# DeltaNet block inverse: crossing products on the two off-diagonal 64x64 array tiles, in banks of their own

## The chip, the cores and the metric

One core of a Trainium2 chip runs the whole program. The metric is the device time of one launch in microseconds (us). The engines are TensorE (PE; its weight loads have rows of their own, PEld), VectorE (DVE), ScalarE (ACT), GpSimd (POOL) and SyncE (SP), which mostly issues transfers. They run side by side and meet only at semaphores.

## The reference, cut to what matters

One inference step of a four-layer trunk in float32. Layers 0 and 3 mix tokens with a bidirectional chunked gated DeltaNet. Per head, per direction and per chunk of 64 tokens it solves a unit lower triangular 64x64 system:

```python
kb = k * beta[..., None]
a = jnp.where(strict, jnp.einsum('bhnid,bhnjd->bhnij', kb, k) * decay, 0.0)
lower = a + jnp.eye(c, dtype=a.dtype)                       # c = 64
rhs = jnp.concatenate([v * beta[..., None], kb * jnp.exp(g)[..., None]], axis=-1)
sol = lax.linalg.triangular_solve(lower, rhs, left_side=True, lower=True, unit_diagonal=True)
```

There are 8 heads of 128 channels. The context tokens (128) and the latent tokens (128) are two groups `g`, each of two chunks, and two directions `d` run over each. So one head has 2 directions x 2 groups x 2 chunks = 8 systems.

## The kernel before

The inverse of each 64x64 matrix is built by doubling. Six levels (`LEV = 6`) take blocks of 1, 2, 4, ... 32 rows to blocks twice as large. For one head the eight matrices lie in tiles of 128 partitions: combination `c = 2*d + g` picks one of four column strips of 64, and the chunk picks the partitions, rows 0 to 63 or 64 to 127. `UT(l, w)[:, 0]` holds the inverse so far (called T here), `UT(l, w)[:, 1]` its transpose (U). `AT` is the system matrix, `MW` the masked product of a level.

The heads go in pairs (`PAIRS = 4`), two heads (h0 and h1 below) at a time, each step for h0 and then for h1. One level is four steps per head:

- `s_w(lev)` (PE, L894): 8 products 64x64, `AT` by T, into PSUM bank `X`. It waits for ACT's copy of T.
- `s_m(lev)` (DVE, L2087): one operation 128x256, the bank times the level's mask, into `MW`.
- `s_ut(lev)` (PE, L902): 8 products that add to T and 8 that add to U, all accumulated in bank `Y`. The last level leaves T out.
- ACT's `s_ut(lev)` (L1586): one copy 128x512 of `Y` into `UT` (128x256 at the first and the last level).

PE's order within a level is s_w h0, s_w h1, s_ut h0, s_ut h1. Every one of these products reads partitions `r` and writes partitions `r`, with `r` the lower or upper half in turn. In the 128x128 array that uses the two diagonal 64x64 tiles (lower to lower, upper to upper) and never the two crossing ones (lower to upper, upper to lower). A float32 product is recorded as two passes, so an operation with 8 products has 16 records.

Around the levels, for the next pair and the one that ends:

- `s_gc` (PE, L855): 8 transposes that spread the decay of the next pair, after level 4. `s_dec` (DVE, L2056) makes 8 operations of it, both heads ahead of `s_m(5)`; ACT's `s_qe` then takes the exponentials.
- `s_kk`, `s_ks` (PE): key products of the next pair, which wait for ACT's last copy of the old one. `s_qd` (DVE, L2070 to L2085): scales them into `AT`, makes the first `MW` in two operations 64x256, one for each half of the partitions (L2079), and the first U. `s_r0` (DVE, L2064) reads bank `ZB` = 1.
- `s_y`, `s_z`, `s_tz`, `s_o` (PE) finish the old pair. `s_z` is the one step whose products cross (a 64x64 block of `AT` from one half into the other half, 128 columns wide); `s_v` (DVE, L2096, L2097) is between `s_tz` and `s_o`. `s_t(h)` (PE) starts T and U of the new pair from `s_qd`'s result.

Every queue is a fixed order written out by hand. The scratch of this stage lies in the weight ring, so that hardly any weights stream while it runs.

Of the kernel before, what the change touches and what calls it, by code (L numbers as in the profile page):

```python
# [7 lines left out]
ALU = mybir.AluOpType  # L8
# [4 lines left out]
P = 128  # L13
# [5 lines left out]
H = 8  # L19
# [10 lines left out]
LEV = 6  # L30
# [135 lines left out]
def trunk(nc, a, outs):  # L166
    y_p, y_s, new_dn, new_k, new_v = outs
    with ExitStack() as ctx:
# [132 lines left out]
        d_dec, d_qd, d_m, d_r0, d_v = (sem("d_" + n) for n in ("dec", "qd", "m", "r0", "v"))  # L301
# [23 lines left out]
        PAIRS, ZB = H // 2, 1  # L325
# [56 lines left out]
        def UT(l, p): return scratch(l, 2560 * p + 1536, 2, 4, HB)  # L382
        def MM(l, p): return scratch(l, 2560 * p + 2048, 4, P)
# [283 lines left out]
        def _(pe):  # L667
# [101 lines left out]
            def deltanet(l):  # L769
# [110 lines left out]
                def utps(Y, half, c, r):  # L880
                    x = HB * (4 * half + c)
                    return ps[r, Y, x:x + HB]

                def s_t(h, w, hd, X, Y):
                    pe.wait_ge(d_qd, hd + 1)
                    pe.wait_ge(a_qe, hd + 1)
                    t = UT(l, w)[:, 1]
                    for c, r in blocks():
                        mm(utps(Y, 0, c, r), t[r, c, :], identc[r, :], c == 0, False, skip_group_check=True)
                    for c, r in blocks():  # L890
                        ins = mm(utps(Y, 1, c, r), identc[r, :], t[r, c, :], False, False, skip_group_check=True)
# [73 lines left out]
                for j in range(PAIRS + 1):  # L965
# [519 lines left out]
        def _(act):  # L1485
# [59 lines left out]
            def deltanet(l):  # L1545
# [991 lines left out]
```

## Time and profile before

| | us |
|---|---|
| median of 3 runs | 2280.64 (2274.31 to 2280.94) |
| the profiled execution, its own time | 2278.45 |
| its span | 2276.6 |
| PE busy | 2180.7 (96%) |
| DVE busy | 736.2 (32%) |
| ACT busy | 390.9 (17%) |
| all 64x64 products at L669, `ring` by `ring`, x4192 records | 180.2 |

The span is one execution as the hardware profiler saw it, and the views below are of it. All times in them count from the span's start. The granted clock of TensorE was 0.983 on average. A PE record lasts some 200 ns because the result has to drain through the array, while the next one starts long before: what a stream of products costs is read from the distance between starts, not from the mean duration.

### The profile page before, as it was taken

The page shows a single profiled execution, that of the slowest core. Times are in us where ns is not written, and L with a number is a line of the kernel's source. Part 1 is how long each engine was busy: PE and PEld are TensorE (multiplying, and loading weights), DVE is VectorE, ACT ScalarE, POOL GpSimd, SP SyncE. Part 2 cuts the span into 40 slices and gives each one's busy share as a digit, 9 for nine tenths or more (in the row PEclk, how much of TensorE's full clock was granted, in tenths as well). Part 3 has the DMA queues.
Part 4 walks back from the last instruction along what each step waited for, and adds up shares of the span by engine and source line. Part 5 has one row for each costly group of instructions (what it writes and reads, how often), then busy time and mean ns, then how long its engine had stood idle before and what let it go on. Part 6 is the DMA issues. An engine that isn't in the chain of part 4 may idle for free.

```text
span 2276.6 us, 44025 instructions
## 1 busy us (share of the span) xinstructions
PE 2180.7 (96%) x19461; PEld 1657.0 (73%) x19461; DVE 736.2 (32%) x1576; ACT 390.9 (17%) x794; POOL 127.1 (6%) x221
## 2 busy tenths in 40 slices
PE   7998989999999999999999999999988899999998
PEld 4776878888888746646687788888878876466465
DVE  2234434777412300000212355562344333000002
ACT  1133441000101000000132210002143330000001
POOL 4000010111000000000000011110000000000000
PEclk8999999999999999999999999999999999999999
DMA  9973029997455699999755799563530057999992
GB/s 337 268 251 101 12 90 322 335 305 257 149 185 194 204 386 383 381 381 379 248 156 191 259 346 286 199 193 95 157 121 7 12 208 256 387 383 380 379 383 113
DMA packets 363975, 550.92 MB, mean 242 GB/s; under 512 B 12176, under 2 KB 312080, under 8 KB 358464
## 3 DMA queue, kind: packets, MB, share of 16 engines
q1 hardware_dynamic: 336288, 466.59, 59.6%
q0 software_dynamic: 21968, 76.84, 10.3%
q10 hardware_dynamic: 5536, 4.73, 0.6%
q8 instruction: 154, 2.52, 0.5%
q14 instruction: 29, 0.24, 0.0%
HBM read 537.64 MB, written 14.93 MB: 243 GB/s over the span
## 4 chain that ended last, share of the span: by engine, by line
PE 76%; SPq 11%; DVE 5%; DMA 4%; ACT 2%; issue 2%; ACTq 0%; DVEq 0%
PE ps L669 73%; SPq L494 7%; SPq L498 3%; DMA work<-in_ada_w 2%; ACT ring L1495 2%; DMA ring<-in_moe_w_down 1%; DVE ring L2056 1%; DVE work L1915 1%; ACT work L1495 1%; DVE ring L2074 0%; DVE ring L2079 0%; DVE ring L2064 0%; DMA ring<-in_ada_w 0%; PE ps L1184 0%; DVE hT L1925 0%
## 5 line engine op out<-in xcount | busy, mean ns | idle before, releaser
L669 PE MATMUL ps<-hT,ring 128*128 128x256 f32 x3200 | 715.7, 383 | 2.9 <-DVE hT L1925 2.5
L669 PE MATMUL ps<-ring,work 128*32 128x384 f32 (+7 forms) x8008 | 693.9, 438 | 17.8 <-ACT work L1495 5.4
L669 PEld LDWEIGHTS ps<-hT,ring 128*128 128x128 f32 x3200 | 609.8, 192 | 115.7 <-issue 21.4
L669 PEld LDWEIGHTS ps<-ring,work 128*32 128x32 f32 (+2 forms) x8008 | 392.6, 115 | 296.9 <-issue 180.6
L1495 ACT ACTIVATE work<-ps 128x256 f32<-128x256 f32 (+6 forms) x220 | 100.5, 467 | 1329.9 <-PE ps L669 1143.8
L669 PE MATMUL ps<-work,ring 128*128 128x256 f32 (+1 forms) x1344 | 283.9, 370 | 0.0
L669 PEld LDWEIGHTS ps<-work,ring 128*128 128x128 f32 (+1 forms) x1344 | 238.6, 185 | 34.0 <-issue 1.7
L2478 DVE SCALAR_TENSOR_TENSOR work<-work,csil 128x1024 f32<-128x1024 f32 x196 | 239.7, 1279 | 39.5 <-DMA work<-in_ada_w 39.3
L669 PE MATMUL ps<-ring 64*64 64x64 f32 (+1 forms) x4192 | 180.2, 230 | 25.4 <-ACT ring L1495 11.1
L669 PEld LDWEIGHTS ps<-ring 64*64 64x64 f32 x4192 | 159.3, 139 | 38.8 <-ACT ring L1495 17.5
L1495 ACT ACTIVATE ring<-ps 128x512 f32<-128x512 f32 (+3 forms) x208 | 101.6, 491 | 306.0 <-PE ps L669 295.8
L669 PE MATMUL ps<-work 128*128 128x128 f32 (+2 forms) x736 | 104.9, 293 | 3.4 <-DVE work L2253 3.3
L669 PEld LDWEIGHTS ps<-work 128*128 128x128 f32 (+1 forms) x736 | 94.0, 199 | 14.3 <-issue 10.3
L2400 DVE TENSOR_TENSOR work<-work,ps 128x384 f32<-128x384 f32 (+1 forms) x24 | 13.3, 553 | 248.6 <-PE ps L669 230.8
L596 POOL DMA_DIRECT2D work<-in_ada_w x112 | 60.2, 538 | 453.4 <-DVE work L2478 260.4
L1933 DVE SCALAR_TENSOR_TENSOR xT<-ps,mods,xT 128x128 f32<-128x128 f32 x160 | 43.6, 343 | 107.8 <-PE ps L669 98.7
L2090 DVE TENSOR_TENSOR ring<-ps,cst 128x256 f32<-128x256 f32 x80 | 33.3, 423 | 93.0 <-PE ps L669 92.7
L1950 DVE TENSOR_SCALAR ring<-ring,par 128x256 f32<-128x256 f32 x48 | 14.8, 352 | 135.2 <-ACT ring L1495 135.2
L669 PE MATMUL ps<-ring,cst 64*64 64x64 f32 (+1 forms) x320 | 46.9, 322 | 8.4 <-ACT ring L1495 8.4
L2461 DVE TENSOR_TENSOR work<-work,ps 128x256 f32<-128x256 f32 x44 | 18.4, 418 | 107.4 <-ACT work L1495 107.4
L2347 DVE COPY work<-ps 128x512 f32<-128x512 f32 x16 | 11.1, 692 | 117.9 <-PE ps L669 117.9
L614 POOL TENSOR_TENSOR tick<-work 1x1 f32<-1x1 f32 x2 | 0.4, 183 | 874.3 <-DMA y_rows<-work 874.3
(266 smaller groups left out, 1076.1 us busy)
## 6 DMA issues: line engine op xcount, KB each, us to landing
ring<-in_moe_w_gu SPq DMA_DIRECT2D x96, 1536.0 KB, 16.0
ring<-in_moe_w_down SPq DMA_DIRECT2D x48, 1536.0 KB, 16.6
work<-in_ada_w POOLq DMA_DIRECT2D x112, 512.0 KB, 6.5
ring<-in_ff_w_gu SPq DMA_DIRECT2D x88, 512.0 KB, 7.7
ring<-in_ada_w SPq DMA_DIRECT2D x40, 1024.0 KB, 8.7
ring<-in_dn_w_in SPq DMA_DIRECT2D x32, 1024.0 KB, 5.5
ring<-in_moe_w_gu SPq DMA_DIRECT2D x32, 1024.0 KB, 8.9
ring<-in_ff_w_down SPq DMA_DIRECT2D x44, 512.0 KB, 9.2
```

What stands on the lines that cost most here:

```text
L494: sp.dma_start(ring[:, x, 0:KC * width].rearrange("p (k n) -> p k n", k=KC), gu[e, :, c:c + width].rearrange("e (k p) n -> p (e k) n", p=P ...
L498: sp.dma_start(ring[:, x, at:at + n * DM].rearrange("p (c n) -> p c n", c=n), dn[e, c * P:(c + n) * P, :].rearrange("e (c p) n -> p (e c) ...
L596: po.dma_start(piece[b], a["ada_w"][third // ADA_T, k * P:(k + 1) * P, c:c + 1024]) \
L669: return pe.matmul(out, lhsT, rhs, start=start, stop=stop, **kw)
L1495: return act.activation(out, in_, fn, **kw)
L1915: tt(mixT[:, 2 * b:2 * b + 2, :], xT[:, 2 * b:2 * b + 2, :], rstd[:, None, :].to_broadcast([P, 2, NT]), ALU.mult).then_inc(d_nx, 1)
L1933: ins = stt(xT[:, k, g * P:(g + 1) * P], ps[:, bank, c * NT + g * P:c * NT + (g + 1) * P], mods[:, l, col + k, g:g + 1], xT[:, k, g * P:(g ...
L1950: ins = ts(v(ys[c]), x, ws[c](tap), None, ALU.mult)
L2056: ins = stt(TT(l, w)[:, 2 * d + g, :], ps4(X)[:, 2 * d + g, :], col(GC, d, g, h), cap[:, d, :], ALU.subtract, ALU.min)
L2090: tt(four(MW(l, w)), ps[:, X, 0:4 * HB].rearrange("p (d g n) -> p d g n", d=2, g=2), level(lev), ALU.mult).then_inc(d_m, 1)
L2461: tt(act_s[:, j % 3, :], gate_s[:, j % 3, :], ps[:, FB[j % 3], NT:2 * NT], ALU.mult) \
L2478: ins = stt(t, piece[b], c, t, ALU.mult, ALU.add)
```

## The change

- In each head one of the two directions is called crossed (`crossed_d`: direction 1 in even pairs, 0 in odd ones), the other straight. For the crossed direction T stays in the half of its own block, while U and `MW` of that block are kept in the other half of the partitions. The products of the crossed direction in `s_w` (T's half to the other) and for T in `s_ut` (the other half back to T's) then run on the crossing array tiles. They are written to a bank of their own, `crossing(p)` = 1 or 4 for h0 or h1, while the straight ones go to `X` and `Y`. The code issues crossing and straight products in turn. The products for U are all on the diagonal tiles as before.
- T of the crossed direction is no longer accumulated in PSUM: DVE adds it (`s_crossed`, 128x128, one per head and level 0 to 4), with a new semaphore `d_t` that `s_w` also waits for. ACT copies 128x384 where it copied 128x512.
- The last copy of U (ACT) puts the crossed blocks back in their own half: three operations, 64x128, 64x128 and 128x128, where there was one of 128x256.
- The first `MW` in `s_qd` takes four operations 64x128 where there were two of 64x256.
- `s_gc` of the next pair moves from after level 4 to after level 3. `s_dec` is split: h0 ahead of `s_m(4)`, h1 ahead of `s_m(5)`.
- Bank numbers move: `X` = 0, 2, 3 or 5, `Y` = 6 or 7, and `ZB` = 4, which is also h1's crossing bank; so `s_t` of h1 waits for `d_r0` too.

```diff
-        PAIRS, ZB = H // 2, 1
+        PAIRS, ZB = H // 2, 4
...
-            return h, 2 * (j % 2) + p, H * DN_LAYERS.index(l) + h, (2, 6)[j % 2] + p, 4 + p
+            return h, 2 * (j % 2) + p, H * DN_LAYERS.index(l) + h, 3 * p + 2 * (j % 2), 6 + p
...
+        def crossed_d(h):
+
+            return 1 - (h // 2) % 2
+
+        def crossing(p):
+            return 3 * p + 1
...
                 def s_t(h, w, hd, X, Y):
                     pe.wait_ge(d_qd, hd + 1)
                     pe.wait_ge(a_qe, hd + 1)
+                    if h % 2:
+                        pe.wait_ge(d_r0, hd + 1)
                     t = UT(l, w)[:, 1]
+                    for c, r, x in crossed(h):
+                        mm(t_crossed(h, c, r), t[x, c, :], identc[x, :])
+                    for n, (c, r) in enumerate(straight(h)):
+                        mm(t_straight(Y, c, r), t[r, c, :], identc[r, :], n < 2, False, skip_group_check=True)
...
                         pe.wait_ge(a_ut, nth(hd, lev - 1, LEV))
-                        for c, r in blocks():
-                            ins = mm(ps[r, X, HB * c:HB * c + HB], AT(l, w)[r, c, r], UT(l, w)[r, 0, c, :])
+                        pe.wait_ge(d_t, nth(hd, lev - 1, LEV - 1))
+                        for (c, r, x), (c2, r2) in zip(crossed(h), straight(h)):
+                            at = HB * (c % 2)
+                            mm(ps[x, crossing(h % 2), at:at + HB], AT(l, w)[r, c, r], t_of(h, w, c, r))
+                            ins = mm(ps[r2, X, at:at + HB], AT(l, w)[r2, c2, r2], t_of(h, w, c2, r2))
...
-                            for c, r in blocks():
-                                mm(utps(Y, 0, c, r), UT(l, w)[r, 1, c, :], MW(l, w)[r, c, :], False, False,
+                            for (c, r, x), (c2, r2) in zip(crossed(h), straight(h)):
+                                mm(t_crossed(h, c, r), UT(l, w)[x, 1, c, :], MW(l, w)[x, c, :])
+                                mm(t_straight(Y, c2, r2), UT(l, w)[r2, 1, c2, :], MW(l, w)[r2, c2, :], False, False,
                                    skip_group_check=True)
...
-                        if lev == LEV - 2 and j + 1 < PAIRS:
+                        if lev == LEV - 3 and j + 1 < PAIRS:
                             both(s_gc, j + 1)
...
+                        if lev < LEV - 1:
+                            x = 4 * HB if lev == 0 else 8 * HB
+                            f(u[:, 2 * HB:x], ps[:, Y, 2 * HB:x], ACT.Copy).then_inc(a_ut, 1)
+                            return
+                        x, y = (2 * HB * (2 + d) for d in (crossed_d(h), 1 - crossed_d(h)))
+                        for r, r2 in zip(ROWS_OF, ROWS_OF[::-1]):
+                            f(u[r, x:x + 2 * HB], ps[r2, Y, x:x + 2 * HB], ACT.Copy)
+                        f(u[:, y:y + 2 * HB], ps[:, Y, y:y + 2 * HB], ACT.Copy).then_inc(a_ut, 1)
...
+                    for d in range(2):
+                        for b, r in enumerate(ROWS_OF):
+                            to = ROWS_OF[1 - b] if d == crossed_d(h) else r
+                            ins = tt(MW(l, w)[to, 2 * d:2 * d + 2], AT(l, w)[r, 2 * d:2 * d + 2, r],
+                                     level(0)[r, d], ALU.mult)
...
+                def s_crossed(lev):
+                    def f(h, w, hd, X, Y):
+                        dve.wait_ge(p_ut, nth(hd, lev, LEV))
+                        t, new = UTF(l, w)[:, 0:2 * HB], ps[:, crossing(h % 2), 2 * HB:4 * HB]
+                        ins = tt(t, t, new, ALU.add) if lev else cp(t, new)
+                        ins.then_inc(d_t, 1)
...
+                        s_crossed(0)(*head(l, j, 0))
                     if j > 0:
                         both(s_v, j - 1)
+                    if j < PAIRS:
+                        s_crossed(0)(*head(l, j, 1))
                     for lev in range(1, LEV if j < PAIRS else 1):
-                        if lev == LEV - 1 and j + 1 < PAIRS:
-                            both(s_dec, j + 1)
+                        if lev >= LEV - 2 and j + 1 < PAIRS:
+                            s_dec(*head(l, j + 1, lev - (LEV - 2)))
                         both(s_m(lev), j)
+                        if lev < LEV - 1:
+                            both(s_crossed(lev), j)
```

DVE, the levels of the first pair in the kernel before: L2090 is `s_m` (the x8 are levels 1 to 4 of both heads), L2056 is `s_dec`.

```order
L2090 TENSOR_TENSOR ring<-ps,cst 128x256 [waits p_w] x8
L2056 SCALAR_TENSOR_TENSOR ring<-ps,sm,cst 128x128 [waits p_gc]
L2056 SCALAR_TENSOR_TENSOR ring<-ps,sm,cst 128x128 x3
L2056 SCALAR_TENSOR_TENSOR ring<-ps,sm,cst 128x128 [waits p_gc]
L2056 SCALAR_TENSOR_TENSOR ring<-ps,sm,cst 128x128 x3
L2090 TENSOR_TENSOR ring<-ps,cst 128x256 [waits p_w] x2
```

The same place in the changed kernel, levels 3 to 5: L2138 is `s_m`, L2146 `s_crossed`, L2101 `s_dec`.

```order
L2138 TENSOR_TENSOR ring<-ps,cst 128x256 [waits p_w] x2
L2146 TENSOR_TENSOR ring<-ring,ps 128x128 [waits p_ut] x2
L2101 SCALAR_TENSOR_TENSOR ring<-ps,sm,cst 128x128 [waits p_gc]
L2101 SCALAR_TENSOR_TENSOR ring<-ps,sm,cst 128x128 x3
L2138 TENSOR_TENSOR ring<-ps,cst 128x256 [waits p_w] x2
L2146 TENSOR_TENSOR ring<-ring,ps 128x128 [waits p_ut] x2
L2101 SCALAR_TENSOR_TENSOR ring<-ps,sm,cst 128x128 [waits p_gc]
L2101 SCALAR_TENSOR_TENSOR ring<-ps,sm,cst 128x128 x3
L2138 TENSOR_TENSOR ring<-ps,cst 128x256 [waits p_w] x2
```

Two more operations stand on DVE between the masks of one level and the next, and four of the eight `s_dec` operations have moved up by one level.

PE, from `s_ut(3)` of h1 to `s_w(4)` of h1 in the changed kernel (the 8 products at L867 are `s_gc`; before, they stood behind the next `s_ut` of h1):

```order
L681 MATMUL ps<-ring 64x64 [waits d_m]
L681 MATMUL ps<-ring 64x64 x15
L867 MATMUL ps<-cst,sm 128x128 x8
L681 MATMUL ps<-ring 64x64 [waits d_t,a_ut]
L681 MATMUL ps<-ring 64x64 x7
L681 MATMUL ps<-ring 64x64 [waits d_t,a_ut]
L681 MATMUL ps<-ring 64x64 x7
```

The count of products is the same. What is new in the rows is the place of L867 and the second semaphore of `s_w`; that half of the products use other array tiles doesn't show in an order.

## Rows read from the trace of the kernel before

**Rows 1.** The page's chain by engine; busy us in stretches, with clock, DMA share, GB/s

```profile
PE 76%; SPq 11%; DVE 5%; DMA 4%; ACT 2%; issue 2%; ACTq 0%; DVEq 0%
...
200.00:300.00 100.00, 88.10 (x2016) 82.00 (x2018) 50.29 (x140) 36.52 (x80) 4.35 (x6) 0.98 0.03 9
1722.00:1822.00 100.00, 88.35 (x2029) 81.63 (x2024) 47.26 (x133) 39.52 (x86) 4.34 (x6) 1.00 0.04 11
```

**Rows 2.** Timeline of one level, first pair of layer 0: start, duration, what [idle before]

```profile
208.37 3.02 PE L669 MATMUL ps<-ring 64*64 64x64 f32 x96 [0.23 <-ACT ring L1495]
...
210.03 0.60 ACT L1495 ACTIVATE ring<-ps 128x512 f32<-128x512 f32 x1 [1.72 <-PE ps L669]
210.97 0.60 ACT L1495 ACTIVATE ring<-ps 128x512 f32<-128x512 f32 x1 [0.34 <-PE ps L669]
211.43 0.42 DVE L2090 TENSOR_TENSOR ring<-ps,cst 128x256 f32<-128x256 f32 x1 [1.91 <-PE ps L669]
211.62 3.02 PE L669 MATMUL ps<-ring 64*64 64x64 f32 x96 [0.23 <-ACT ring L1495]
```

**Rows 3.** Timeline of PE where `s_z` (64x128) and `s_t` (64x64) meet

```profile
227.50 0.76 PE L669 MATMUL ps<-ring 64*64 64x128 f32 x10 [0.92 <-DVE ring L2064]
228.00 0.27 PE L669 MATMUL ps<-cst,ring 64*64 64x64 f32 x2
228.10 0.28 PE L669 MATMUL ps<-ring 64*64 64x128 f32 x2
228.11 0.28 PE L669 MATMUL ps<-cst,ring 64*64 64x64 f32 x4
228.21 0.28 PE L669 MATMUL ps<-ring 64*64 64x128 f32 x2
228.22 0.28 PE L669 MATMUL ps<-cst,ring 64*64 64x64 f32 x4
```

**Rows 4.** Timeline of all engines from the end of level 4 to `s_kk`

```profile
217.34 1.09 PE L855 MATMUL ps<-cst,sm 128*128 128x128 f32 x8
...
218.03 2.16 DVE L2056 SCALAR_TENSOR_TENSOR ring<-ps,sm,cst 128x128 f32<-128x128 f32 x8 [2.02 <-PE ps L855]
218.35 1.01 PEld L669 LDWEIGHTS ps<-ring 64*64 64x64 f32 x32 [0.17 <-issue]
...
220.10 0.74 DVE L2090 TENSOR_TENSOR ring<-ps,cst 128x256 f32<-128x256 f32 x2
...
221.74 2.05 PE L669 MATMUL ps<-work 128*128 128x128 f32 x16
```

**Rows 5.** Timeline of DVE between two pairs, and the masks that start two pairs

```profile
223.00 1.13 DVE L2074 SCALAR_TENSOR_TENSOR ring<-ps,sm,ring 128x128 f32<-128x128 f32 x4 [2.15 <-PE ps L669]
224.16 0.85 DVE L2079 TENSOR_TENSOR ring<-ring,cst 64x256 f32<-64x256 f32 x2
...
231.94 0.68 DVE L2097 TENSOR_TENSOR ring<-ps,sm 128x512 f32<-128x512 f32 x1
236.26 0.89 DVE L2090 TENSOR_TENSOR ring<-ps,cst 128x256 f32<-128x256 f32 x2 [3.65 <-PE ps L669]
239.34 0.42 DVE L2090 TENSOR_TENSOR ring<-ps,cst 128x256 f32<-128x256 f32 x1 [2.18 <-PE ps L669]
...
267.41 0.89 DVE L2090 TENSOR_TENSOR ring<-ps,cst 128x256 f32<-128x256 f32 x2 [3.65 <-PE ps L669]
```

**Rows 6.** Groups by line and shape, 196 to 330 us (busy, mean ns), and ACT's four `s_z` copies

```profile
L2079 DVE TENSOR_TENSOR ring<-ring,cst 64x256 f32<-64x256 f32 x16 | 6.7, 420 | 0.4
...
L1495 ACT ACTIVATE ring<-ps 128x512 f32<-128x512 f32 x40 | 23.9, 597 | 45.4 <-PE ps L669 45.4
L1495 ACT ACTIVATE ring<-ps 128x256 f32<-128x256 f32 x30 | 11.3, 376 | 14.7 <-PE ps L669 14.5
...
317.11 1.56 ACT L1495 ACTIVATE ring<-ps 64x256 f32<-64x256 f32 x4 [1.27 <-PE ps L669]
```

**Rows 7.** Busy us (as in the first group) in the stretch before the first pair's levels

```profile
198.20:205.00 6.80, 4.23 (x82) 4.04 (x78) 4.23 (x13) 0.77 (x2) 0.00 (x0) 0.50 0.04 14
```

More of the change, by code:

```diff
@@ L300, in trunk @@
         d_gate, d_fin, d_nx = sem("d_gate"), sem("d_fin"), sem("d_nx")
-        d_dec, d_qd, d_m, d_r0, d_v = (sem("d_" + n) for n in ("dec", "qd", "m", "r0", "v"))
+        d_dec, d_qd, d_m, d_r0, d_v, d_t = (sem("d_" + n) for n in ("dec", "qd", "m", "r0", "v", "t"))
         d_max, d_p, d_pt = (sem("d_" + n) for n in ("max", "p", "pt"))
@@ L878, in blocks, with crossed, straight, t_straight @@
                             yield c, slice(HB * b, HB * b + HB)
-                def utps(Y, half, c, r):
-                    x = HB * (4 * half + c)
-                    return ps[r, Y, x:x + HB]
+                def crossed(h):
+                    for c in range(2 * crossed_d(h), 2 * crossed_d(h) + 2):
+                        for b in range(2):
+                            yield c, ROWS_OF[b], ROWS_OF[1 - b]
+                def straight(h):
+                    for c in range(2 - 2 * crossed_d(h), 4 - 2 * crossed_d(h)):
+                        for b in range(2):
+                            yield c, ROWS_OF[b]
+                def t_straight(Y, c, r):
+                    x = HB * (2 + c % 2)
+                    return ps[r, Y, x:x + HB]
+                def t_crossed(h, c, r):
+                    x = HB * (2 + c % 2)
+                    return ps[r, crossing(h % 2), x:x + HB]
+                def u_of(Y, c, r):
+                    return ps[r, Y, HB * (4 + c):HB * (5 + c)]
+                def t_of(h, w, c, r):
+                    return UT(l, w)[r, 0, t_at(h, c), :]
                 def s_t(h, w, hd, X, Y):
@@ L1588, in g @@
                         act.wait_ge(p_ut, nth(hd, lev, LEV))
-                        first = 256 if lev == LEV - 1 else 0
-                        last = 256 if lev == 0 else 512
-                        f(UT(l, w).rearrange("p u c n -> p (u c n)")[:, first:last], ps[:, Y, first:last],
-                          ACT.Copy).then_inc(a_ut, 1)
+                        u = UTF(l, w)
+                        if lev < LEV - 1:
[6 more added lines that the diff above has]
+                        f(u[:, y:y + 2 * HB], ps[:, Y, y:y + 2 * HB], ACT.Copy).then_inc(a_ut, 1)
                     return g
@@ L2076, in s_qd @@
                     link(ins)
-                    for b in range(2):
-                        r = slice(HB * b, HB * b + HB)
-                        ins = tt(four(MW(l, w))[r], four(AT(l, w))[r, :, :, r], level(0)[r], ALU.mult)
+                    for d in range(2):
[3 more added lines that the diff above has]
+                                     level(0)[r, d], ALU.mult)
                     link(ins)
@@ L2089, in f @@
                         dve.wait_ge(p_w, nth(hd, lev - 1, LEV - 1))
-                        tt(four(MW(l, w)), ps[:, X, 0:4 * HB].rearrange("p (d g n) -> p d g n", d=2, g=2), level(lev),
-                           ALU.mult).then_inc(d_m, 1)
+                        b = min(X, crossing(h % 2))
+                        tt(four(MW(l, w)), ps[:, b:b + 2, 0:2 * HB].rearrange("p d (g n) -> p d g n", g=2),
+                           level(lev), ALU.mult).then_inc(d_m, 1)
+                    return f
+                def s_crossed(lev):
[4 more added lines that the diff above has]
+                        ins.then_inc(d_t, 1)
                     return f
```

10 lines of the change are left out of this document (6 added, 4 removed).

## The prediction, made before the changed kernel ran

> **What bounds the kernel now.** I read the page's chain first. TensorE is 76% of it, and the windows over the two DeltaNet stages show PE at 88% with DMA at 3 to 4% [rows 1]. So nothing streams beside these stages: what they lose or gain moves everything behind them by the same amount, also the later stages that wait for weights.
>
> Next the timeline of one level. PE starts a group of 96 records at 208.37 and the next at 211.62, so a level of two heads takes 3.24 us [rows 2]. The 96 records are 48 pairs, one record on each diagonal tile; (3.02 - 0.22)/48 = 58 ns a pair (0.22 is the drain of the last). The group holds `s_w` of h1 (8 pairs, 0.47), `s_ut` of h0 (16 pairs, 0.93), `s_ut` of h1 (0.93), and `s_w` of h0 for the next level, which hides under ACT's copy for h1. ACT starts at 210.03, where 0.47 + 0.93 of issue ended at 209.77: 0.26 from the last start to a reader's start. Its copy ends at 211.57 and PE starts at 211.62: 0.05 for a hand-over. The loop that sets the level is therefore h1's: 0.47 + 0.93 + 0.93 + 0.26 + 0.60 + 0.05 = 3.24. It is PE's issue for 2.8 us and a wait of 0.4.
>
> Between two pairs it is another engine. DVE runs from 223.00 to 232.6 without a wait [rows 5], and `s_o` stands behind `s_v` at its end. One whole pair takes 267.41 - 236.26 = 31.15 us [rows 5]. There are four pairs in each of two layers.
>
> **The levels.** The change puts half of the `s_w` products and a quarter of those of `s_ut` on the crossing tiles. Per head, `s_w` then needs 4 groups of four records and `s_ut` 4 such groups for T and 8 pairs for U. Whether four records, two of which share their rows of the array with the other two, cost 58 ns as two do is the main question, and the trace answers part of it. `s_z` is on the crossing tiles, `s_t` on the diagonal ones, and from 228.00 on both run: pairs of `s_z` start at 228.10 and 228.21, 0.11 apart, as a 128 wide product needs, and in between `s_t` sends its 4 records (two pairs) every 0.11 us, 228.11 and 228.22 [rows 3]. Both keep the pace they have alone. So I take 58 ns for four: `s_w` 0.23, `s_ut` 0.23 + 0.47 = 0.70. An upper bound is the density seen there, 6 records in 0.11 us or 18 ns a record, thus 72 ns for four. A lower one is 58: the same tiles can't be faster than alone.
>
> The Trainium skill has a rule against this: in "TensorE: Matmul & The Clock Gate", Part 3 (row/col tiling), a weight load overlaps matmuls in flight only when its row group differs, and a crossing tile has the row group of a diagonal one. By that rule the crossing products would gain nothing (the second rival gives its time). "TensorEngine Tiling (Array Packing)", Key Properties, says the opposite, that different tiles load and multiply in parallel. The trace goes with the latter [rows 3].
>
> PE's issue for a level falls to 2 x 0.93 = 1.87 us, and it is no longer the bound. Late next is one head's own chain: `s_w` 0.23, 0.26, mask 0.42 [rows 2], 0.05, `s_ut` 0.70, 0.26, ACT's copy, 0.05. The copy of 384 columns lies between 376 ns for 256 and 597 for 512 [rows 6]: 0.49. Sum 2.46, so a level gives 0.78. `s_crossed` (128 columns, by the same slope 0.42 - 0.13 = 0.29) starts with ACT's copy and ends before it. DVE's four operations are 1.4 us in 2.46, so it is free in time. Level 1 takes 239.34 - 236.26 = 3.08 now [rows 5] and also 2.46 then: 0.62.
>
> **From the mask of level 3 to `s_kk`.** Now 221.74 - 211.43 = 10.31 us [rows 2, 4]. After, counted from the start of the mask of h0: 0.47 with hand-over, two `s_ut` 1.40, end at 1.87. `s_gc` now stands here; it keeps PE from its `s_ut` to the next `s_w` for 1.10 (the last product of `s_ut` at 217.25, `s_gc` at 217.34, `s_w` at 218.35) [rows 4]. It used to hide nothing and does not now. `s_w(4)` starts at 2.97, done 3.46. `s_dec` of h0 starts 0.69 after `s_gc` (218.03 - 217.34), at 2.65, and takes 4 x 0.26 = 1.04 (8 take 220.10 - 218.03 = 2.07) [rows 4]; the mask of level 4 queues behind it on DVE and starts at 3.69, not 3.46. Then 0.47, `s_ut` twice 1.40: 5.56. `s_crossed` of h1 from 5.82 to 6.1, `s_dec` of h1 to 7.15, and only then the mask of level 5, although `s_w(5)` was long done. 0.47, U of h0 0.47, 0.26: ACT at 8.35. Its three-part copy: 64-partition copies of opposite halves don't overlap, four took 1.56, 0.39 each with 256 columns [rows 6], so 0.28 with 128, three 0.83. `s_kk` at 9.23. The stretch gives 10.31 - 9.23 = 1.08. Halving `s_dec` on the path gives 1.04 of it.
>
> **From `s_kk` to the next first mask.** DVE is the bound here, so each of its additions counts. `s_qd` has two 64x256 in 0.85, 0.43 each [rows 5, 6]; four of 64x128 are 4 x 0.30 = 1.2: +0.33, for both heads +0.66. The copy `s_crossed(0)` of h0 stands ahead of `s_v`, and `s_o` waits for `s_v`: +0.20 queued (bounds 0.13 by columns alone, 0.34 with its whole latency). That of h1 comes after `s_v`, under `s_o`. PE's `s_t` gets 0.23 shorter under this cover, worth nothing. `s_w(1)` of h0 gives 0.23. Sum +0.63. The new waits (`d_t` at `s_w`, `d_r0` at `s_t` of h1) find their semaphores set: `s_r0` is done before `s_z`, which is ahead of `s_t` of h1 on PE.
>
> **The sum.** A pair with a successor: -0.62 (level 1) - 0.78 (level 2) - 1.08 + 0.63 = -1.85 us, 31.15 to 29.3. Three a layer: -5.6. The last pair: -0.62 - 3 x 0.78 + 0.2 for the three-part copy = -2.8. The start of the first pair: +0.66 on DVE against 0.23 and 0.23 on PE, which count double because the clock is at half there [rows 7]: about 0. Per layer -8.4, twice -16.7. The profiled execution's 2278.45 becomes 2261.8; it is 2.2 below the median, so against 2280.64 I forecast **2264 us**. With 72 ns for four records each chain grows by 8 x 14 ns = 0.11 a level, 40 levels 4.5 us: 2268. With cheaper small DVE operations and a `s_dec` that hides wholly, some 4 us less: 2260. Together with the spread of the runs (2274 to 2281 before) this case is 2257 to 2272.
>
> **Rivals.**
>
> *Crossing tiles add no rate.* Then `s_w` and `s_ut` keep 0.47 and 0.93. A level gives only ACT's 0.11, as h1's loop stays the bound. Levels 2 to 4 give 0.33 by that. Around `s_dec`, half of whose 2.07 us leaves the path, I count 0.85 gained, and 0.45 lost to the three-part copy (0.83 for 0.38). Between the pairs +0.66 and +0.20 are lost. So a pair is -0.33 - 0.85 + 0.45 + 0.86, about +0.15, a layer with the +0.66 of its start and -0.25 of its last pair +0.9, in all +1.7: 2282. For it: only one place in the trace has both kinds of tile, and with 6 records in 0.11 us, not 8. Against: both streams there lose nothing.
>
> *Clock.* The granted clock was 0.50 from 198.20 to 205.00, after PE had idled for more than 2 us twice behind `s_qd` [rows 7]. That is the 1.2 GHz level; in the rest of the stage it was 2.4. The change widens PE's idle time between pairs by some 0.9 us and leaves holes of 0.3 in the levels. At half clock a head's chain grows by 0.93 to 3.4 us, about 0.28 us lost per us. One such stretch of 6.8 us at each of six boundaries costs 11: 2275. That is a loss of gain, not of time.
>
> *Slower.* Products on tiles of both kinds might exclude each other altogether, so that alternating them also breaks the overlap of the diagonal pair. Four records then take 233 ns. At 58 the gain is 16.7, at 117 it is -1.7; it turns at about 110 ns. Beyond, each ns costs 16 groups a level: (233 - 117) x 16 = 1.86 us, over about 36 levels 67: 2349. Against it is that `s_z` and `s_t` interleave without a loss [rows 3].
>
> *The change doesn't reach the end time.* The stage could end earlier and the next wait for weights. DMA is idle through both stages [rows 1], so the loads start when they end. I give this little.
>
> **Chances.** Forecast 0.68; no added rate 0.12; clock 0.09; slower 0.05; other, on either side, 0.06. Differences under 0.3% (6.8 us) can't be told from none. Faster by more: 0.68 + 0.03 + 0.03 = 0.74; within: 0.16; slower: 0.10. The range 2256 to 2281 holds the forecast's case and the clock's and cuts the second rival's.
>
> **What would show it.** In the timeline after: 64x64 records of both kinds four to 58 ns in `s_w` (8 products issued in 0.23), a level in 2.46, ACT's copy as the last wait before `s_w`, masks of level 5 starting right behind `s_dec`, DVE without a wait from `s_qd` to `s_v`, a pair in 29.3. The forecast is wrong if `s_w` of 8 products still takes 0.47, if stretches at 0.50 appear in the levels, or if `s_w` ends up waiting for `d_t`.

## The result and the profile after

The median fell from 2279.1 us (2274.31 to 2280.94) to **2265.32 us** (2262.47 to 2276.62), six runs each: the medians differ by 13.8 us. The ratio over all the runs is 0.9946 with a 95% interval of 0.9932 to 0.9960: 0.54% less, or 12.3 us. The prediction was 2264.

The profiled execution of the changed kernel took 2262.47, with a span of 2260.6, 16.0 less than that of before. The page, first the busy times, then the chain:

```profile
PE 2148.5 (95%) x19461; PEld 1622.0 (72%) x19461; DVE 761.1 (34%) x1688; ACT 388.6 (17%) x826; POOL 127.1 (6%) x221
...
PE 72%; SPq 10%; DVE 7%; DMA 6%; issue 2%; ACT 2%; ACTq 0%; POOL 0%; DVEq 0%
```

PE's share of the chain fell from 76% to 72% and DVE's rose from 5% to 7% [rows 1]: what PE gave up was not all found, some of it is now DVE's. The timeline of the second pair of layer 0 holds the levels, which answer to [rows 2]: start, us, engine, line, operation, and in brackets the idle time before and what ended it.

```profile
236.84 0.49 ACT L1535 ACTIVATE ring<-ps 128x384 f32<-128x384 f32 x1 [0.21 <-PE ps L681]
236.84 0.29 DVE L2146 TENSOR_TENSOR ring<-ring,ps 128x128 f32<-128x128 f32 x1 [0.41 <-PE ps L681]
237.21 0.43 DVE L2138 TENSOR_TENSOR ring<-ps,cst 128x256 f32<-128x256 f32 x1
237.38 2.28 PE L681 MATMUL ps<-ring 64*64 64x64 f32 x96 [0.24 <-ACT ring L1535]
...
238.66 0.49 ACT L1535 ACTIVATE ring<-ps 128x384 f32<-128x384 f32 x1 [1.33 <-PE ps L681]
...
239.74 0.42 DVE L2138 TENSOR_TENSOR ring<-ps,cst 128x256 f32<-128x256 f32 x1
239.91 1.99 PE L681 MATMUL ps<-ring 64*64 64x64 f32 x80 [0.24 <-ACT ring L1535]
```

The same 96 records now take 2.28 us instead of 3.02, and masks and groups repeat every 2.53. What PE waits for last is still ACT's copy, now 0.49 long. `s_crossed` starts with it and ends 0.20 sooner.

The first pair of each layer didn't get that. The clock was at its 1.2 GHz level from 200.0 to 206.9 and from 1691.6 to 1698.5, and the first masks stand at 204.33 and 1696.56. When it fell at 200.0, PE had waited 2.53 us up to 197.58 and stood again in a wait of 3.74. So level 1 of these two pairs took 3.30 and 3.15 us. Before, the same happened in layer 3 only: there such a stretch reached from 1700.0 to 1710.3 and level 1 took 4.24, while in layer 0 it ended at 205.0, just ahead of the first mask at 205.11. The row of the first stretch holds start and end, length, busy us of PE, PEld, DVE, ACT and POOL with their counts, then clock, DMA share and GB/s:

```profile
200.00:206.90 6.90, 4.58 (x120) 4.42 (x122) 4.10 (x12) 0.77 (x2) 0.00 (x0) 0.51 0.01 2
```

The rest of the second pair answers to [rows 4] and [rows 5]:

```profile
242.51 1.13 DVE L2101 SCALAR_TENSOR_TENSOR ring<-ps,sm,cst 128x128 f32<-128x128 f32 x4 [0.28 <-PE ps L867]
...
242.84 0.69 PE L681 MATMUL ps<-ring 64*64 64x64 f32 x32
243.56 0.74 DVE L2138 TENSOR_TENSOR ring<-ps,cst 128x256 f32<-128x256 f32 x2
...
245.90 1.12 DVE L2101 SCALAR_TENSOR_TENSOR ring<-ps,sm,cst 128x128 f32<-128x128 f32 x4
...
246.94 0.74 DVE L2138 TENSOR_TENSOR ring<-ps,cst 128x256 f32<-128x256 f32 x2
...
247.41 1.15 PE L681 MATMUL ps<-ring 64*64 64x64 f32 x32 [0.71 <-DVE ring L2138]
...
248.13 1.71 ACT L1535 ACTIVATE ring<-ps 64x128 f32<-64x128 f32 x6 [0.18 <-PE ps L681]
249.03 2.05 PE L681 MATMUL ps<-work 128*128 128x128 f32 x16 [0.48 <-ACT ring L1535]
```

Two of these rows show the array tiles at work in one kernel. At 242.84 `s_w` of both heads is 32 records on all four tiles: 0.69, less 0.22 of drain is 0.47, or 59 ns for four records. At 247.41 U of both heads is 32 records on the two diagonal tiles: 1.15 - 0.22 = 0.93, 58 ns for two.

Of the profiled execution's 16.0 us, the stage of layer 0 (first `s_kk` to the start of the last record of `s_o`) gave 6.5, that of layer 3 gave 7.5, and the rest of the program 2.0: -0.6 ahead of the first stage, -3.5 between the two, +2.1 behind. The code of that rest is the same, and its time varies: over the profiled executions of the thirteen kernels told of here it was 191.2 to 194.8 us ahead of the first stage, 1367.2 to 1375.2 between the two and 449.0 to 453.9 behind. The medians differ by less than the two profiled executions, mostly because the profiled one of after is the fastest of its six.

### The profile page after: what moved, and what is told of

It is laid out like the page before. It is cut to its first block, busy times and chain, and to the rows that moved or that the text cites. A ratio compares the mean times of both kernels' runs of the same rounds, so it can differ in the third digit from the quotient of the medians.

```text
span 2260.6 us, 44249 instructions
## 1 busy us (share of the span) xinstructions
PE 2148.5 (95%) x19461; PEld 1622.0 (72%) x19461; DVE 761.1 (34%) x1688; ACT 388.6 (17%) x826; POOL 127.1 (6%) x221
## 3 DMA queue, kind: packets, MB, share of 16 engines
q8 instruction: 154, 2.52, 0.5%
## 4 chain that ended last, share of the span: by engine, by line
PE 72%; SPq 10%; DVE 7%; DMA 6%; issue 2%; ACT 2%; ACTq 0%; POOL 0%; DVEq 0%
PE ps L681 70%; SPq L506 7%; SPq L510 3%; DMA work<-in_ada_w 3%; DMA ring<-in_moe_w_down 2%; ACT ring L1535 1%; DMA ring<-in_dn_w_in 1%; DVE work L2539 1%; DVE ring L2125 1%; DVE ring L2119 1%; DVE ring L2101 1%; DVE work L1960 1%; ACT work L1535 1%; DVE ring L2129 0%; DVE ring L2109 0%
## 5 line engine op out<-in xcount | busy, mean ns | idle before, releaser
L681 PE MATMUL ps<-ring 64*64 64x64 f32 (+1 forms) x4192 | 154.7, 236 | 32.0 <-ACT ring L1535 9.4
L681 PEld LDWEIGHTS ps<-ring 64*64 64x64 f32 x4192 | 131.8, 139 | 47.5 <-ACT ring L1535 16.8
L1535 ACT ACTIVATE ring<-ps 128x384 f32<-128x384 f32 (+5 forms) x240 | 100.0, 419 | 294.5 <-PE ps L681 284.2
L1997 DVE SCALAR_TENSOR_TENSOR ring<-ring,par 128x256 f32<-128x256 f32 x96 | 42.3, 482 | 1.7
```

What stands on the lines that cost most here:

```text
L681: return pe.matmul(out, lhsT, rhs, start=start, stop=stop, **kw)
L1535: return act.activation(out, in_, fn, **kw)
L1997: ins = stt(v(ys[c]), x, ws[c](tap), v(ys[c]), ALU.mult, ALU.add)
```

## The experiments

The unit below is the **pair**: the time between the first masks (level 1, h0) of two successive pairs of heads; of the kernel before 31.15, of the changed one 29.52 and 29.45 for the second and third pair of layer 0. The first pair of a layer is longer (30.36 and 30.09), since its level 1 ran at the lower clock. "Masks 3 to 5" is from the mask of level 3 to that of level 5, both of h0, in the second pair of layer 0: 8.67 before, 7.20 after. PE sometimes stands still and waits for nothing but its own instructions (more in the last section). Such a wait adds 0.2 to 1.0 us to single pairs, and each kernel has one trace, so a few tenths in a single pair prove little. Medians of before were 2279.04, 2278.54, 2279.04 and 2279.49 in the four groups of runs.

### Do the crossing tiles add a rate of their own?

In the changed kernel every crossed product reads and writes the same half, as the straight ones do:

```
-  mm(t_crossed(h, c, r), t[x, c, :], identc[x, :])
+  mm(t_crossed(h, c, r), t[r, c, :], identc[r, :])
...
-  mm(ps[x, crossing(h % 2), at:at + HB], AT(l, w)[r, c, r], t_of(h, w, c, r))
+  mm(ps[r, crossing(h % 2), at:at + HB], AT(l, w)[r, c, r], t_of(h, w, c, r))
...
-  mm(t_crossed(h, c, r), UT(l, w)[x, 1, c, :], MW(l, w)[x, c, :])
+  mm(t_crossed(h, c, r), UT(l, w)[r, 1, c, :], MW(l, w)[r, c, :])
```

> The changed kernel, but every crossing product reads and writes its own half, so it runs on a diagonal tile (12 places per head and level: the products of the crossed direction; they read the wrong half, so the numbers differ from the reference's). Counts, banks, waits, ACT's and DVE's work stay. Theory (the four array tiles work side by side, and this is the gain): s_w goes from 0.23 back to 0.47 us and s_ut from 0.70 to 0.93, a level from 2.52 to about 3.13 us, a pair from 29.52 to about 31.3 us, the whole about +17 us to the changed kernel, so within 0.3% of the kernel before. Rival (the gain is ACT's shorter copy and the moved s_gc and s_dec): the level stays at 2.5 us, the whole within 3 us of the changed kernel.

Measured: a level 3.11 to 3.18, a pair 32.05, time 2285.39 (8 runs), ratio 1.0034 (1.0023 to 1.0045). In its timeline ACT is free again well ahead of PE's result, and the masks of h0 are 3.11 apart:

```profile
240.13 0.89 DVE L2138 TENSOR_TENSOR ring<-ps,cst 128x256 f32<-128x256 f32 x2 [3.46 <-PE ps L681]
...
242.77 0.49 ACT L1535 ACTIVATE ring<-ps 128x384 f32<-128x384 f32 x1 [0.44 <-PE ps L681]
...
243.24 0.42 DVE L2138 TENSOR_TENSOR ring<-ps,cst 128x256 f32<-128x256 f32 x1 [0.18 <-PE ps L681]
```

Only the tiles differ from the changed kernel, and they are worth 0.65 us a level, 2.5 a pair and 20 us in all. Without them everything else in the change is a loss of 0.34%.

### Does the order of the products matter?

```
-                        for (c, r, x), (c2, r2) in zip(crossed(h), straight(h)):
+                        for c, r, x in crossed(h):
                             at = HB * (c % 2)
                             mm(ps[x, crossing(h % 2), at:at + HB], AT(l, w)[r, c, r], t_of(h, w, c, r))
+                        for c2, r2 in straight(h):
+                            at = HB * (c2 % 2)
                             ins = mm(ps[r2, X, at:at + HB], AT(l, w)[r2, c2, r2], t_of(h, w, c2, r2))
```

> The changed kernel with the crossing products of s_w and of T issued first, four in a row, then the four straight ones, in place of in turn. Theory (each array tile has its own line of work, as s_z and s_t showed before the change): straight products overtake, s_w still 0.23 to 0.3 us, the level 2.5 to 2.65 us. Rival (tiles work side by side only where neighbours in the order differ): s_w 0.47 us, the level about 3.1 us, the whole +15 us.

Measured (one run, 2269.84): a level 2.58 instead of 2.52, pairs 29.64 to 30.18 (the first of each layer 30.80 and 30.85); the one of 30.18 has a wait of 0.33 for instructions. So the four tiles overlap even when the issue isn't in turn; turns are worth 0.05 to 0.06 a level.

### What is the move of s_gc and s_dec worth?

Alone, on the kernel before:

```
-  if lev == LEV - 2 and j + 1 < PAIRS:
+  if lev == LEV - 3 and j + 1 < PAIRS:
       both(s_gc, j + 1)
...
-  if lev == LEV - 1 and j + 1 < PAIRS:
-      both(s_dec, j + 1)
+  if lev >= LEV - 2 and j + 1 < PAIRS:
+      s_dec(*head(l, j + 1, lev - (LEV - 2)))
```

> The kernel before with only the move: s_gc after level 3, s_dec of h0 ahead of the masks of level 4, of h1 ahead of those of level 5. Theory: it gives about 0.85 us a pair here, 31.15 to 30.3, six pairs -5 us. Rival: PE is the bound of a level in this kernel, so s_gc only changes its place and nothing is gained: 31.15 us a pair, 0 us.

Measured: pair 30.38, masks 3 to 5 7.48, time 2272.79 (10 runs), ratio 0.9971 (0.9962 to 0.9981). The theory held: 0.77 a pair where it wanted 0.85. The same two edits undone in the changed kernel:

> The changed kernel with s_gc back after level 4 and all eight operations of s_dec ahead of the masks of level 5. Theory: 8 operations (2.07 us) stand again between s_gc and the masks of level 5 where 4 (1.04) did: +1.04 us a pair with a successor, 29.52 to 30.56, six such pairs +6.3 us. Rival (the place doesn't matter, since s_dec of h0 delays the masks of level 4 instead): a pair stays at 29.5 us, the whole within 1 us in the trace.

Measured: masks 3 to 5 7.63 instead of 7.20, pairs from 29.72 to 30.9, time 2267.23 (4 runs), ratio 0.9951 (0.9935 to 0.9968). Neither the theory's +1.04 nor the rival's 0 came: the pair is 0.2 to 0.4 longer (29.93 and 29.72 where the changed kernel has 29.52 and 29.53), and 0.18 of the 7.63 is a level of 2.70 without any side work in it. The two intervals overlap, so the whole program doesn't show the difference. So the same move gives 1.2 us in that stretch in the kernel before, and 0.2 to 0.4 in the changed one. Undone, `s_dec` is one block and PE waits for the mask behind it:

```profile
244.73 2.16 DVE L2101 SCALAR_TENSOR_TENSOR ring<-ps,sm,cst 128x128 f32<-128x128 f32 x8 [0.29 <-PE ps L867]
...
247.27 1.15 PE L681 MATMUL ps<-ring 64*64 64x64 f32 x32 [1.52 <-DVE ring L2138]
```

Why the move is worth so much less in the changed kernel stands in the rows of DVE. In the kernel before with the move alone, the second half of `s_dec` follows the masks of level 4 at once and is over more than 1 us before the mask of level 5:

```profile
246.14 1.11 DVE L2056 SCALAR_TENSOR_TENSOR ring<-ps,sm,cst 128x128 f32<-128x128 f32 x4
...
248.41 0.42 DVE L2090 TENSOR_TENSOR ring<-ps,cst 128x256 f32<-128x256 f32 x1 [1.15 <-PE ps L669]
```

From the masks of level 4 to the first of level 5 it is 3.08 there, not more than a level without side work (3.25). In the changed kernel the two `s_crossed` of level 4 stand ahead of this half on DVE, and that of h1 waits for PE's `s_ut` of h1. So the half starts at 245.90 only, right behind `s_crossed` of h1 (245.69), and holds up the masks: 3.38, where a bare level has 2.52. Whether PE's issue or one head's chain bounds the level doesn't explain this: in the run on the same tiles, where the level is bound by PE's issue again (3.18), `s_crossed` stands at the same place and the step takes 3.89:

```profile
253.45 0.29 DVE L2146 TENSOR_TENSOR ring<-ring,ps 128x128 f32<-128x128 f32 x1 [0.65 <-PE ps L681]
253.65 1.12 DVE L2101 SCALAR_TENSOR_TENSOR ring<-ps,sm,cst 128x128 f32<-128x128 f32 x4
```

No run moved `s_dec` of h1 ahead of `s_crossed` and nothing else; the spread version below does it among other things.

One half of the move alone, `s_gc` early as in the changed kernel and all of `s_dec` late:

```
-  if lev >= LEV - 2 and j + 1 < PAIRS:
-      s_dec(*head(l, j + 1, lev - (LEV - 2)))
+  if lev == LEV - 1 and j + 1 < PAIRS:
+      both(s_dec, j + 1)
```

> The changed kernel with s_gc after level 3 as it is, but all eight operations of s_dec ahead of the masks of level 5. It splits the move in two. Theory: from the mask of level 3 to that of level 5 the changed kernel takes 3.82 + 3.38 = 7.20 us and e2_gc_late 7.63; here the masks of level 4 wait for s_gc on PE only (3.5 us for that step) and those of level 5 for eight operations (3.38 + 1.04 - 0.2 for the later start = 4.2 us): 7.7 us, as e2_gc_late, so the gain of the move is the split of s_dec. Rival: the sum stays at 7.2 us, since what level 4 gets back is worth as much.

Measured (one run, 2284.06): masks 3 to 5 8.56, in which PE has a wait of 0.34 for instructions; in layer 3 they take 8.06 to 8.14. Neither value was right. Two nearly whole costs added to two bare levels give it: from the mask of level 3 to that of level 4 it is 3.63 (layer 3, second pair), 1.11 over a bare level for `s_gc` on PE, and from there to level 5 it is 4.42, 1.90 over it for the 2.07 of `s_dec` on DVE. That is a reading made afterwards. The next two runs test it. Of the whole program's 19 us over the changed kernel some 5 come from the clock (last section).

`s_gc` alone split by head, h0 after level 2 and h1 after level 3:

```
-  if lev == LEV - 3 and j + 1 < PAIRS:
-      both(s_gc, j + 1)
+  if lev - 2 in (0, 1) and j + 1 < PAIRS:
+      s_gc(*head(l, j + 1, lev - 2))
```

> The changed kernel with s_gc alone split by head: h0 after level 2, h1 after level 3. s_dec stays as changed, four operations ahead of the masks of level 4 and four ahead of those of level 5. Masks 3 to 5 of h0 take 7.20 us now. Theory A (s_gc and s_dec lie beside each other, and s_dec takes over as soon as s_gc is gone): s_dec of h0 then starts behind s_crossed(3) of h1 instead of behind the transposes, 0.2 to 0.3 earlier; masks 3 to 5 take 6.9 to 7.0. Theory B (s_gc on PE hides nothing and costs its 1.10, as the prediction took it): masks 3 to 5 take 6.1 to 6.3. A pair is 29.5 now: A 29.2 to 29.3, B 28.4 to 28.6.

Measured (one run, 2263.05): masks 3 to 5 6.77, but the level before them went from 2.53 to 3.14. Its cause stands on PE:

```profile
240.98 0.65 PE L867 MATMUL ps<-cst,sm 128*128 128x128 f32 x4
...
241.56 0.69 PE L681 MATMUL ps<-ring 64*64 64x64 f32 x32
```

The next level's `s_w` comes 0.58 behind the first transpose, where two `s_ut` and `s_w` follow each other without a gap otherwise. Four transposes cost 0.62 here, so PE's 0.24 of idle time is no room for them, and the pair is 29.69, not less than 29.5. Both theories failed in part: the early half of `s_dec` did take over some of the room, but `s_gc` hides nothing, as the prediction had it.

Then also `s_dec`, one operation at a time behind the masks and `s_crossed`, and ACT's `s_qe` by head:

```
+  steps = [s_m(lev), s_m(lev)] + ([s_crossed(lev)] * 2 if lev < LEV - 1 else [])
+  for k, step in enumerate(steps):
+      step(*head(l, j, k % 2))
+      n = 3 * (lev - 2) + k
+      if j + 1 < PAIRS and lev > 1 and k < 3 and n < 8:
+          dec_part(l, j + 1, n)
```

> The changed kernel with three moves: s_gc split by head, h0 after level 1 and h1 after level 2; s_dec split into its eight single operations, three in each of levels 2 and 3 (one behind each mask, one behind s_crossed of h0) and two in level 4; ACT's s_qe one head at a time, ahead of its level 4 and level 5 copies. Nothing is left out. Masks 3 to 5 of h0 take 7.20 us in the changed kernel where two bare levels would be 5.04, so 2.16 us a pair are s_gc and s_dec together. Theory A (they cost only because of where they stand): DVE waits 0.28 to 0.41 behind each mask and behind s_crossed of h0, and one operation of 0.27 fits there; PE idles 0.24 beyond its drain of 0.22 in each level, and four transposes of 0.11 fit. Levels stay 2.5 to 2.65, a pair is 27.4 to 27.8, and the span is 10 to 13 us under that of the changed kernel: 2248 to 2251. Theory B (each operation on DVE costs its time wherever it stands, as the prediction took it): 8 x 0.27 stays, only s_gc's 1.1 can go, a pair is 28.4 or more, span 2254 or more.

Measured: pairs of 28.60 and 28.61 where no step is longer than its work explains (the others 28.86 to 30.6), time 2258.94 (2 runs), ratio 0.9911 (0.9891 to 0.9931), span 2256.0. A level of this kernel:

```profile
241.91 0.42 DVE L2148 TENSOR_TENSOR ring<-ps,cst 128x256 f32<-128x256 f32 x1 [0.71 <-PE ps L681]
242.25 0.34 DVE L2102 SCALAR_TENSOR_TENSOR ring<-ps,sm,cst 128x128 f32<-128x128 f32 x1
...
242.51 0.41 DVE L2148 TENSOR_TENSOR ring<-ps,cst 128x256 f32<-128x256 f32 x1
242.84 0.34 DVE L2102 SCALAR_TENSOR_TENSOR ring<-ps,sm,cst 128x128 f32<-128x128 f32 x1
...
243.35 0.29 DVE L2156 TENSOR_TENSOR ring<-ring,ps 128x128 f32<-128x128 f32 x1 [0.18 <-PE ps L681]
243.56 0.34 DVE L2102 SCALAR_TENSOR_TENSOR ring<-ps,sm,cst 128x128 f32<-128x128 f32 x1
...
244.42 0.42 DVE L2148 TENSOR_TENSOR ring<-ps,cst 128x256 f32<-128x256 f32 x1
```

Three operations of `s_dec` stand in this level and it takes 2.51, the same as a bare one: `s_dec` became free. The levels with transposes in front take 3.15, here too some 0.6 more for four of them. So of the 2.16 us that the changed kernel spends over two bare levels, 1.24 are `s_gc` (2 x 0.62) and the 0.92 left went: 29.52 - 28.60 = 0.92. Theory A holds for `s_dec`, B for `s_gc` (the pair of 28.60 alone would fit B's 28.4 or more too; the rows of the single levels decide); the span fell by 4.6 us where A wanted 10 to 13. Whether the size of the pieces, their place ahead of `s_crossed` or ACT's part did it wasn't taken apart.

### What bounds the part between two pairs?

```
        s_qd(*head(l, j, 1))
-       s_crossed(0)(*head(l, j, 0))
    if j > 0:
        both(s_v, j - 1)
    if j < PAIRS:
-       s_crossed(0)(*head(l, j, 1))
+       both(s_crossed(0), j)
```

> The changed kernel with the 128x128 copy s_crossed(0) of h0 behind s_v on DVE, not ahead of it. Theory (DVE bounds the stretch between two pairs and each of its operations ahead of s_v counts): -0.20 us a pair, 29.52 to 29.32. Rival (PE or ACT bounds it): no change in the pair.

Measured (one run, 2262.99): from `s_kk` to the next first mask it is 14.97 in all six pairs, against 15.17 in the changed kernel: 0.20 each, as DVE's bound wants. Two whole pairs without further waits are 29.26 and 29.31, against 29.45 and 29.53.

### A version with shorter levels

T of both directions is no longer accumulated in PSUM. It goes to `X` and the crossing bank, one DVE operation 128x256 adds it to T for both directions, ACT copies U alone (128x256), and U of h1 is issued behind the next `s_w` of h0. Core of the edit:

```
-                            f(u[:, 2 * HB:x], ps[:, Y, 2 * HB:x], ACT.Copy).then_inc(a_ut, 1)
+                            f(u[:, 4 * HB:8 * HB], ps[:, Y, 4 * HB:8 * HB], ACT.Copy).then_inc(a_ut, 1)
...
-                        t, new = UTF(l, w)[:, 0:2 * HB], ps[:, crossing(h % 2), 2 * HB:4 * HB]
-                        ins = tt(t, t, new, ALU.add) if lev else cp(t, new)
+                        b = min(X, crossing(h % 2))
+                        t = UTF(l, w)[:, 0:4 * HB].rearrange("p (d n) -> p d n", d=2)
+                        tt(t, t, ps[:, b:b + 2, 2 * HB:4 * HB], ALU.add).then_inc(d_t, 1)
...
-                        both(s_w(lev), j)
-                        both(s_ut(lev), j)
+                        s_w(lev)(*h0)
+                        if lev > 1:
+                            s_uu(lev - 1)(*h1)
+                        s_w(lev)(*h1)
```

> A version of my own on top of the changed kernel: T of both directions is no longer accumulated in bank Y but written to X and the crossing bank and added by DVE in one operation 128x256 per head and level; ACT copies only U (128x256), off the chain; the products for U of h1 stand behind s_w of h0 of the next level; the first T is copied by ACT. Theory: the level is bound by a chain that no longer holds ACT's copy and the 0.47 us of U: s_w 0.23 + 0.26 + mask 0.42 + 0.05 + T 0.23 + 0.26 + sum 0.42 + 0.05 = 1.92, with DVE's queue 2.0 to 2.1 us, from 2.52; a pair from 29.5 to about 27.7, the whole about -14 us to the changed kernel, 2251. Rival (DVE becomes the bound, four operations of 0.42 and their hand-overs): 2.3 us a level or more, the whole -5 us or less.

Measured: a level 2.03, a pair 27.99 to 28.85, time 2255.32 (4 runs), ratio 0.9898 (0.9881 to 0.9914). The level came as the theory had it. The pair missed its 27.7 and the time its 2251, with masks 3 to 5 at 6.4 to 7.2 and waits for instructions in them. Then QE's product on GpSimd instead of DVE:

```
-  dve.wait_ge(a_qe, hd + 1)
-  tt(QE(l, w), QE(l, w), qT[:, h, None, P:NT].to_broadcast([P, 2, P]), ALU.mult)
...
+  po.wait_ge(a_qe, hd + 1)
+  po.tensor_tensor(QE(l, w), QE(l, w), qT[:, g, None, P:NT].to_broadcast([P, 2, P]), ALU.mult).then_inc(o_z, 1)
```

> e6_t_added, and the product of QE and q at the end of s_qd (128x256, one per head) moves from DVE to GpSimd, which has nothing to do there; s_o waits for it. Theory (DVE bounds the stretch between two pairs): two operations less ahead of s_v, 0.33 us each in the queue, so -0.66 us a pair, 28.5 to 27.9 where no wait on instruction supply falls into it, six pairs -4 us: about 2251. Rival (something else comes due, or GpSimd slows DVE): no change in the pair.

Measured: from `s_kk` to the next first mask 14.30 in all six pairs, against 14.97: 0.67 where 0.66 of DVE's time was taken away. A pair is 27.0 to 27.7 (the first 28.7), some 1.0 less; what goes beyond 0.67 lies in the levels, where the waits for instructions are longer in the version before. Time 2252.44 (4 runs), ratio 0.9888 (0.9872 to 0.9905): the interval overlaps with the one before, so the gain is shown by the trace and not by the times. Last, with the three moves of the spread `s_dec`:

> e7 (T of both directions added outside PSUM, QE's product on GpSimd) with the three moves of e9. In e7 a level is 2.03 and masks 3 to 5 take 6.86, 2.8 over two levels. DVE has 4 x 0.42 = 1.68 of work in a level now; three operations of 0.27 make it 2.5 in levels 2 and 3 and two make it 2.2 in level 4, 1.2 over three bare levels. If that sum holds, a pair gives 1.6 us against e7 (27.5 to 25.9), six pairs 9.6, and the span is 2241, the time about 2243. If the small operations cost more between the large ones, or PE waits for instructions as in e6 (0.7 to 1.0 us once or twice a pair), a pair is 26.5 to 27 and the time 2247 to 2250.

Measured: levels 2.68, 2.68, 2.28, 2.28, a pair 26.8 to 27.7 (the first 28.5), time **2249.67 us** (2247.64 to 2252.93, 4 runs), ratio 0.9870 (0.9854 to 0.9887). It beats both kernels, by 1.3% and 0.7%. The steps from the first mask to that of level 5 gave 1.0 us in the second pair (9.92 for 10.92, in which the version without the spread has a wait for instructions), the pair only 0.2 (means of five pairs each, 27.19 for 27.42). Part of the gain is lost at the end of the pair:

```profile
243.97 0.42 DVE L2177 TENSOR_TENSOR ring<-ps,cst 128x256 f32<-128x256 f32 x1 [0.17 <-PE ps L688]
...
245.22 0.62 ACT L1561 ACTIVATE ring<-ring 128x512 f32<-128x512 f32 x1
245.74 2.11 ACT L1561 ACTIVATE ring<-ps 128x256 f32<-128x256 f32 x7
247.04 2.05 PE L688 MATMUL ps<-work 128*128 128x128 f32 x16 [0.70 <-ACT ring L1561]
```

From the mask of level 5 to `s_kk` it is 3.07, where the kernel without the spread has 2.27 (245.13 to 247.40): `s_qe` of h1 now starts 1.25 after that mask and stands on ACT ahead of the last copies. The four pairs that follow have 2.54 to 2.56, against 2.26. That `s_qe` is the cause is read from its place and wasn't tested.

## Why the prediction was right, and where its steps were off

Forecast -16.7 for the profiled execution, measured -16.0; 2264 for the median, measured 2265.3. The mechanism was right: the crossing tiles add a rate of their own, and they are the whole gain. By its steps:

- **Four records in 58 ns**: 59 measured, and confirmed by the run on the same tiles. Here the two pages of the Trainium skill disagreed: by the rule in "TensorE: Matmul & The Clock Gate", Part 3, as the prediction read it, the crossing products should have gained nothing, and they did gain (2.52 us a level against 3.18 without them). "TensorEngine Tiling (Array Packing)", Key Properties, agrees with the runs.
- **A level in 2.46**: 2.52. The terms were right (mask, two waits of about 0.26, `s_ut`, ACT's copy of 0.49); the hand-overs were 0.06 short. Level 1 gave 0.56 for 0.62, level 2 0.71 for 0.78, each later level of the last pair likewise.
- **Mask of level 3 to `s_kk` in 9.23**: 9.24 to 9.44, 9.29 in the second pair. The path was right step by step (mask of level 4 after 3.69, measured 3.82; mask of level 5 after 7.15, measured 7.20), but the reason given for the gain was wrong. "Halving `s_dec` on the path gives 1.04 of it": undoing the move costs 0.2 to 0.4. On the same tiles, with the move in place, the stretch takes 10.37, as long as before (10.31). So the tiles gave 1.08 of it, and all the rest of the change nothing. The sentence took the 2.07 of `s_dec` as fully exposed before and half as exposed after. Before, the step from the mask of level 4 to that of level 5 took 2.18 over a level (5.43 for 3.25) and the 8 transposes are 1.1 of that, so `s_dec` cost about 1.1. After, its second half costs 0.86 behind `s_crossed` of h1 and its first half 0.2: as much.
- **`s_kk` to the next first mask, +0.63**: 14.52 became 15.17, +0.65. That DVE bounds it was shown twice, by the copy behind `s_v` (-0.20) and QE's product on GpSimd (-0.67).
- **A pair -1.85**: -1.63 and -1.70 in layer 0, -1.62 and -1.50 in layer 3 for the second and third pairs. The small misses above add up to it. The first pairs gave -0.79 and -2.23: level 1 ran at the lower clock after the change in both layers (3.30 and 3.15), and before it in layer 3 only (4.24). The prediction had one level 1 for all pairs.
- **The start of the first pair, about 0**: `s_kk` to the first mask went from 12.26 to 12.12 and from 12.25 to 12.12, -0.14 and -0.13.
- **The last pair -2.8**: 24.71 became 22.49 from its first mask in layer 0, -2.2, and 24.70 became 22.68 in layer 3, -2.0; in layer 0 its last mask came 0.26 late behind a wait of PE for instructions. The stages gave 14.0 where 16.7 were forecast; the other 2.0 of the profiled -16.0 can't be put down to the change. So the match to 0.7 us is in part luck. The match of the median is too: the forecast took 16.7 off a median of 2280.64, six runs gave 2279.1 for it, and the medians differ by 13.8.

**The rivals.** *No added rate* was excluded by the run on the same tiles, which is that rival built. Its price was mis-sized: 31.30 a pair and 2282 forecast, 32.05 and 2285.4 measured. The failed term is the 0.85 for `s_dec`: masks 3 to 5 fell from 8.67 to 8.27 only, because the second half of `s_dec` stands behind `s_crossed`. Alone in the kernel before, the move did give 0.77. *Clock*: the prediction named stretches at 0.50 in the levels as a sign of being wrong. There was one in level 1 of each layer's first pair, which cost 0.78 and 0.63 us there; none fell into the other levels or at the six boundaries where the rival wanted them. The granted clock was 0.986 on average after 0.983. *Slower* by exclusion of the tiles: excluded by the same rows. *The end time doesn't move*: it moved.

## What to carry to other kernels

Small float32 products gain from all four 64x64 array tiles only if every operand lies in the half that the tile wants. Price the restructuring without the gain first: here it cost 0.34%, and the tiles gave 0.9%. Side work on another engine is free where it fits into a wait of that engine: four operations as a block behind the masks of level 4 in the kernel before, single ones in the changed kernel. It isn't free behind an operation that itself waits late, as `s_crossed` does. So a new operation in a queue also changes what the work behind it costs. Side work on the issuing engine was not free: 0.62 us for four transposes.

## What was not expected of the hardware

**PE waits for instructions.** In the version with T added, PE stands still with nothing to wait for but its own instructions:

```profile
239.88 1.09 PE L868 MATMUL ps<-cst,sm 128*128 128x128 f32 x8 [0.68 <-issue]
```

Its weight loads' waits of this kind between 225 and 330 us sum to 1.6 us before, 1.3 on the same tiles, 2.3 in the changed kernel and 5.6 in this version, and the places differ from pair to pair (0.56 in the spread one, 0.34 in the one with `s_dec` late). In these traces, one for each kernel, there are more of them where PE gets through its products faster. What feeds or starves it was not tested.

**The clock fell once in a pair** in the kernel with all of `s_dec` late. In the others it was at 0.50 around the start of each stage, and within the pairs once more only with `s_gc` late. Windows of it, columns as in the row on the clock above:

```profile
250.00:254.40 4.40, 2.16 (x71) 1.73 (x66) 3.02 (x11) 2.99 (x9) 0.00 (x0) 1.00 0.01 4
254.40:257.80 3.40, 3.20 (x15) 3.21 (x16) 1.02 (x4) 0.96 (x4) 0.00 (x0) 0.50 0.00 0
```

PE was busy for 2.16 of 4.40 us ahead of it, with a wait of 1.74 for the masks of level 5, and `s_kk` then ran at the 1.2 GHz level: its 16 records took 3.56 instead of 2.05. From `s_kk` to the next first mask it is up to 16.08 then, not 15.17: 0.5 to 0.9 us a pair. That is the prediction's clock rival, at one move's distance from the changed kernel. The kernel with `s_gc` late waited 1.52 at that place and its `s_kk` ran at full clock there (2.05); in its first pair it had one such stretch. Which difference decides stays open.
